# A delta-rule recurrence in turns: the gram and its masks ahead of the level additions, the transposes behind scan_sa

## What is computed

```
def step(S, inp):                       # for each position t, each head
    r_t, w_t, k_t, v_t, kk_t, a_t = inp
    sa = einsum('bhvk,bhk->bhv', S, -kk_t)
    S  = S * w_t + sa (x) (kk_t * a_t) + v_t (x) k_t
    y_t = einsum('bhvk,bhk->bhv', S, r_t)
...
mod = silu(cond) @ w_ada + b_ada        # second block: shift, scale, gate
```

## Time and profile before

| | |
|---|---|
| median of 3 runs | 788.23 us (784.02, 788.23, 788.24) |
| profiled execution, its own time | 784.26 us |
| its span, first to last instruction | 782.4 us |
| mean granted clock of TensorE | 0.986 |
| TensorE busy | 743.0 us (95%) |
| VectorE, ScalarE, GpSimd busy | 448.6, 307.3, 172.5 us |
| turns -1 to 14 of the recurrence | 264.3 to 403.3 us |

### The profile page before, as it was taken

The page is one execution under the profiler, slowest core; times in us unless marked ns, Lnnn a source line. Parts: engine busy times, 40 slices in busy tenths (PEclk is TensorE's granted clock), DMA queues, the critical chain, the costliest instruction groups (busy, mean ns, idle before and its releaser), DMA issues.

```text
span 782.4 us, 17629 instructions
## 1 busy us (share of the span) xinstructions
PE 743.0 (95%) x7606; PEld 607.3 (78%) x7606; DVE 448.6 (57%) x801; ACT 307.3 (39%) x644; POOL 172.5 (22%) x132
## 2 busy tenths in 40 slices
PE   3999999999999988889899999999999999999997
PEld 2488888777777767778788888877777777776897
DVE  4863734777999323355754433849655756664711
ACT  5634443566632122233333436423225434434300
POOL 1344330000144312323321000840000000004651
PEclk9999999999999999889999999999999999999999
DMA  8033225224175885330003235122302121133131
GB/s 256 28 108 87 78 78 162 81 81 93 34 172 108 202 286 164 111 109 5 4 3 125 92 108 133 48 81 82 107 3 78 32 74 33 55 95 102 61 108 54
DMA packets 116765, 72.83 MB, mean 93 GB/s; under 512 B 26832, under 2 KB 114128, under 8 KB 116688
## 3 DMA queue, kind: packets, MB, share of 16 engines
q1 hardware_dynamic: 98496, 65.12, 28.5%
q10 hardware_dynamic: 18192, 6.58, 3.4%
HBM read 64.35 MB, written 7.34 MB: 92 GB/s over the span
## 4 chain that ended last, share of the span: by engine, by line
PE 81%; DVE 9%; DMA 3%; issue 3%; ACT 1%; SPq 1%; POOLq 0%; POOL 0%; ACTq 0%; DVEq 0%
PE bank L530 19%; PE bank L999 9%; PE bank L524 6%; PE bank L526 6%; PE bank L525 6%; DVE arena L1683 3%; PE bank L1040 2%; PE bank L1023 2%; PE bank L643 2%; PE bank L549 2%; PE bank L675 2%; PE bank L778 2%; PE bank L692 2%; PE bank L1133 1%; PE bank L1135 1%
## 5 line engine op out<-in xcount | busy, mean ns | idle before, releaser
L530 PE MATMUL bank<-arena 128*128 128x256 f32 x736 | 165.1, 382 | 0.0
L530 PEld LDWEIGHTS bank<-arena 128*128 128x128 f32 x736 | 138.1, 190 | 24.7 <-issue 7.0
L2068 POOL TENSOR_TENSOR w_lo<-arena,w_hi 128x1024 fp32r<-128x1024 f32 x24 | 59.2, 2466 | 179.5 <-ACT w_hi L1250 179.5
L1250 ACT ACTIVATE w_hi<-arena 128x1024 fp32r<-128x1024 f32 x44 | 46.4, 1057 | 88.3 <-DMA arena<-w_in 87.0
L524 PE MATMUL bank<-x_hi,w_hi 128*128 128x512 f32 x192 | 77.1, 402 | 0.0
L526 PE MATMUL bank<-x_hi,w_lo 128*128 128x512 f32 x192 | 75.8, 395 | 0.0
L525 PE MATMUL bank<-x_lo,w_hi 128*128 128x512 f32 x192 | 75.7, 394 | 0.0
L2164 POOL COPY arena<-arena 128x512 f32<-128x512 f32 x4 | 2.4, 612 | 186.9 <-DVE arena L1975 186.9
L524 PEld LDWEIGHTS bank<-x_hi,w_hi 128*128 128x128 f32 x192 | 36.3, 189 | 9.1 <-issue 1.4
L526 PEld LDWEIGHTS bank<-x_hi,w_lo 128*128 128x128 f32 x192 | 36.3, 189 | 8.4
L525 PEld LDWEIGHTS bank<-x_lo,w_hi 128*128 128x128 f32 x192 | 36.4, 190 | 7.9
(11 more groups left out here) (268 smaller groups left out, 1634.9 us busy)
## 6 DMA issues: line engine op xcount, KB each, us to landing
arena<-w_in SPq DMA_DIRECT2D x45, 512.0 KB, 4.0
arena<-w_ada SPq DMA_DIRECT2D x12, 1024.0 KB, 5.9
arena<-w_in SPq DMA_DIRECT2D x8, 1024.0 KB, 5.5
arena<-w_out SPq DMA_DIRECT2D x8, 1024.0 KB, 5.1
lt_dram<-arena ACTq DMA_DIRECT2D x16, 256.0 KB, 2.4
arena<-x SPq DMA_DIRECT2D x4, 512.0 KB, 5.6
arena<-x SPq DMA_DIRECT2D x1, 2048.0 KB, 7.8
out<-arena SPq DMA_DIRECT2D x8, 256.0 KB, 2.9
```

What stands on the lines that cost most here:

```text
L530: last = mm(o, lhs(k), rhs(k), start=(k == 0), stop=(k == n - 1))
L1250: A(WHI[n % 3][:, :], WR[n % 3][:, 0:1024], ACT.Copy).then_inc(weights_rounded, 1)
L2068: TT(WLO[n % 3][:, :], WR[n % 3][:, 0:1024], WHI[n % 3][:, :].bitcast(f32), SUB)\
```

## The change

Four edits of order; no operation is added, removed or resized.

1. TensorE: gram(g+2) moves up from behind the growth to the place of turned(g+1), and turned(g+1) moves down behind scan_sa(g-1).
2. ScalarE: copy_turned(g+1) moves behind copy_sa(g-1) (and behind the copy of a piece at slot 0).
3. VectorE: the two mask_gram(g+2) move ahead of the level additions add_x.
4. The pieces of modulation: one each in turns -1 to 4 at slot 0, and two each in turns 5, 6 and 7. Before, turns 0, 1 and 2 had two each and turns 3 to 7 one each at slot 1.

```
@@ MODS_BY
-        for n, (g, k) in enumerate([(-1, 0), (0, 0), (0, 1), (1, 0), (1, 1), (2, 0), (2, 1), (3, 1), (4, 1), (5, 1), (6, 1), (7, 1),
+        for n, (g, k) in enumerate([(-1, 0), (0, 0), (1, 0), (2, 0), (3, 0), (4, 0), (5, 0), (5, 1), (6, 0), (6, 1), (7, 0), (7, 1),
                                     (8, 0)]):
@@ TensorE, the loop over turns
                     project_y(0, 0, g - GROUPS + 1)
-                if nxt:
-                    turned(g + 1)
+                if 0 <= g < GROUPS - 2:
+                    gram(g + 2)
                 mods_here(g, 0)
                 if nxt:
                     grow(g + 1, 0)
                 if now:
                     grow(g, 1)
-                if 0 <= g < GROUPS - 2:
-                    gram(g + 2)
                 if old:
                     scan_sa(g - 1)
+                if nxt:
+                    turned(g + 1)
                 mods_here(g, 1)
                 mods_here(g, 2)
@@ ScalarE
                     copy_rhs(g - 1)
-                if nxt:
-                    copy_turned(g + 1)
                 copy_mods(g, 0)
                 if old:
                     copy_sa(g - 1)
+                if nxt:
+                    copy_turned(g + 1)
                 copy_mods(g, 1)
@@ VectorE
                     update(g - 2)
+                if 0 <= g < GROUPS - 2:
+                    for h in range(2):
+                        mask_gram(g + 2, h)
                 if nxt:
                     add_x(g + 1, 0)
                 if now:
                     add_x(g, 1)
-                if 0 <= g < GROUPS - 2:
-                    for h in range(2):
-                        mask_gram(g + 2, h)
```

## The result

The changed kernel takes 777.4 us (median of 4 runs, 775.5 to 781.8), the kernel before 787.2 us beside it: ratio 0.9889, 95% interval 0.9854 to 0.9924. A second measurement of the same changed kernel gave 776.1 us and 0.9872 (0.9843 to 0.9901). So it is 1.1 to 1.3% faster. Forecast were 782 us and a gain of 6.0 us; measured are about 10 us.

What follows compares the result with a forecast made beforehand. TensorE was taken as full nearly everywhere, so only its idle and half-clock time in the recurrence could be won. 3.0 + 0.6 + 2.45 - 0.1 = 6.0 us off the 788.2 us median gave 782 us, range 773 to 792.

Steps and rivals of the forecast that it cites:

- the first case: Whole kernel: 777 to 786 us, the forecast together with the rival of instructions hidden throughout; chance 0.50.
- rival 1: Turns 4 and 7: fewer load collisions, both stalls and their low clock go, 9.8 us more, 772 us; chance 0.17.
- rival 3: Nothing moves: the mask's wait becomes issue in full, the w_ada wait returns at turn 2; 787 us, chance 0.15.
- the prediction's own sign: Turns 1 to 8: the total is wrong if the issue sum or low-clock time changes by over 3 us.
- (a): Turns 9 to 13: earlier gram and masks remove the mask wait and part of turn 11's waits; 4.0 us gained.
- (b): Turns 9 to 13: instruction supply takes 1.0 us back, leaving 3.0 of 4.0; bounds 4.0 and 1.5.
- (c): Transposes behind scan_sa, copies behind copy_sa: masks covered by 0.6 us, nothing lost; 0.6 us gained before turn 0's head.
- (d): Turn 0: moved modulation pieces remove the 1.05 us w_ada wait and 1.4 us from low clock; 2.45 gained, minus 0.1.
- (e): Turns 1 to 8: weight loads against instruction packets, set at 0; bounds gain 12.3 or loss 9.8 us.

Runs made afterwards that it cites:

- e2: Changed kernel with the old table of modulation pieces, so the three edits of order alone; 781.4 us, ratio 0.9964 to the kernel before.
- e5: Changed kernel with the transposes done three times over in turns 9 to 13, 128 more small TensorE records a turn; 785.4 us, ratio 0.9987.
- e6: Changed kernel with one added matmul over 512 columns (4 TensorE records) ahead of the transposes in turns 9 to 13; 778.7 us, ratio 0.9896.
- e3: Kernel before with the twelve w_ada and three w_out blocks loading only their first eighth; 769.3 us, ratio 0.9810.
- e1: Kernel before with only the new table of modulation pieces; 779.1 us, ratio 0.9958.
- e8: Changed kernel with the last twelve of fifteen weight blocks loaded in two halves, the second issued when the first landed; 774.7 us, ratio 0.9852.
- e9: Changed kernel with the last thirteen weight blocks loaded in two halves, the second issued when the first landed; 775.6 us, ratio 0.9879.

## Why the prediction was right, and where it was not

The sign, the range and the effect of most edits held; the total was 5 us high, and two of its terms were wrong in opposite directions. That 777.4 us lies in the range is in part luck: it stands on the border between the first case and rival 1, and what happened is rival 1's mechanism in turns 4 and 7 together with rival 3's in turns 9 to 13. By the prediction's own sign the sum is wrong, for low-clock time moved by 10 us where 3 were allowed.

- **(a), the waits.** Right in the main: L675 no longer waits for L1722, turn 11's wait for the transposes' copies (L1372) is gone, and the additions are in time (0.2 us for L1756 in turn 0, nothing after). Wrong for turn 11: of its 1.3 us I kept 0.3, but the wait for L1747 did not shrink at all (0.8 us for 0.7).
- **(b), the instruction supply.** This is the step that failed. It let 1.0 us of 4.0 come back; about all of it came back. The issue waits in turns 9 to 13 went from 1.1 to 3.6 us, TensorE's busy time rose by 0.6, and the stretch went from 39.4 to 40.3 us (39.7 the second time, 39.0 in e2). The term of 3.0 us measured -0.9 to +0.4. The pessimistic bound of 1.5 (1.8 by its own terms, 4.0 less twice 1.1) was too high as well. I read "most packets show no stall" as slack, but a packet that comes in just as it is wanted shows no stall either; that this is so here is my reading, which e5 and e6 support. Rival 3 was right about these turns. The Trainium skill's rule that crossing a block is mostly hidden ("Runtime: NRT & Kernel Launch", section "Instruction fetch mechanics") doesn't hold here: e5 and e6 have equal busy time and differ by 3.6 us.
- **(c).** Right: 0.2 us, in turn 11 only. The gain of 0.6 us ahead of turn 0 measured 0.5.
- **(d).** The w_ada wait of turn 0 went, and turn 0 fell from 9.0 to 5.4 us, a piece less included. But the low clock only moved: turn 1 has a 3.4 us issue stall, 7 us at the low clock begin behind it, and the turn takes 12.2 instead of 9.6 us although it too has a piece less. Turns 0 and 1 together took 18.6 us before and 17.6 after, and two pieces of 1.07 us or more left them, so nothing of the 2.45 us can be seen there. In e6, without the low clock, they took 13.8.
- **(e), loads against packets.** Set at 0 with bounds -12.3 and +9.8. The large stalls with low clock of turns 4 and 7 went (rival 1's mechanism), one in turn 1 came. Over turns -1 to 8 issue waits fell by 1.2 us (6.5 to 5.3), and time at the low clock by 10 us, worth 4.3, of which (d) had counted 1.4. So the term came to about 4 us, and it is this that made up for (b). e3 shows that the loads cause the stalls; that the new schedule meets less of them had a chance of 0.17, as rival 1, and why it does is not explained.
- **Why both parts are needed.** The prediction priced them apart and added them up. e1 shows that they aren't independent: the new table takes away the pieces that covered the mask, and e1 pays 5.4 us for it in turns 1 to 5, which the new order saves. Together they gained 1.1 to 1.3%, each alone 0.4%; the intervals are too wide to say that the whole is more than the sum.

Still open: why the stretches at the low clock differ so between the kernels. With small loads the old order still had 10 us of it and the new one none, though neither has a long stall; whether the order or its idle time in turns -1 to 1 decides was not tried. A stall alone doesn't decide: 0.7 us of idle time stood ahead of e3's stretch, and 2.2 us in e6 had none behind them. Open too is which loads hit which packets and why; e8 and e9 show only that shorter loads move the collision.

## What to carry to other kernels

Where TensorE runs hundreds of small matmuls, count the records beside the microseconds, and before pricing a wait that is to go, ask whether the instructions behind it are already there: a profile with an "issue" stall at every third packet can be near its limit at the others too, as turns 9 to 13 were. Large loads beside such a stretch hold up its instructions, and a stall that they cause can cost nearly as much again at the low clock; moving them to where matmuls are wide is the thing to try, which no run here did. Where loads wait for each other, add up the whole chain. Price parts of a change together when one removes the cover that the other provides.

## What the runs showed of the hardware

- A weight load holds up TensorE's instructions: with an eighth of the traffic, issue waits of turns -1 to 8 fell from 6.5 to 0.7 us and the kernel gained 14.6 us, far more than the 1.0 us for which it had visibly waited for weights.
- Each of the 21 issue stalls between 255 and 425 us, before and after, ended 2.2 to 2.9 us after the start of a 16 KB instruction packet.
- The same instructions up to turn 8 took 84.7, 84.9 and 85.0 us in three profiles and 80.9 in a fourth (e6), which had a stall of 2.2 us instead of 3.3 to 3.6 and no low clock.
- Equal busy time of TensorE, 40.65 and 40.51 us, took 47.1 us as small records and 43.5 us as wide ones.
- Thirteen 1 MB blocks in four parts each, every part waited for, brought 24.6 us of waits for w_ada where whole loads brought none; a part of 256 KB of w_ada landed in 2.9 us in the median, a whole block of the changed kernel in 5.6.
